# Scans without their empty ends, an output projection that begins with high parts, and two sums moved in the last FFN group

## The chip, the cores and the metric

The kernel is one program on one core of a Trainium2 chip. The metric is the device time of one execution in microseconds (us), median of three runs, lower is better. The engines are TensorE (PE, with its weight loads as PEld), VectorE (DVE), ScalarE (ACT), GpSimd (POOL) and SyncE (SP, which only issues DMAs here).

## The reference, cut to what matters

Two layers of a hybrid encoder trunk on x of shape 1 x 1024 x 1024, all in float32. One input projection feeds three mixers: a bidirectional Mamba-2 scan (8 heads of 64, state 128, chunks of 128 tokens, so 8 chunks), a gMLP spatial gate and a dilated attention. Their outputs are concatenated, go through an output projection, and a depthwise-conv gated FFN of width 2816 follows.

```python
def ssd_chunked(x, dt, a_neg, bm, cm):        # per direction; the backward one runs on flipped inputs
    ...
    states = jnp.einsum('bcsgn,bcsgh,bcsghp->bcghpn', bc, decay_out, xdt)
    def step(h, inp):
        st, dec = inp
        return h * dec[..., None, None] + st, h       # each chunk sees the state BEFORE it
    h0 = jnp.zeros((b, g, hg, p, n), jnp.float32)
    _, prev = lax.scan(step, h0, (states, chunk_decay))
    y_off = jnp.einsum('bctgn,bcghpn,bctgh->bctghp', cc, prev, jnp.exp(acs))
    return (y_diag + y_off)
...
y = y_fwd + y_bwd + d_skip * xs
y = rmsnorm(y * silu(z), out_gain)
x = x + concat(y_ssd, y_gmlp, y_attn) @ w_out
x = x + (silu(gate) * val) @ w_down                   # gate, val = dwconv(rmsnorm(x) @ w_up)
```

The state that the first chunk of a direction sees is zero, and the state after its last chunk is used by nobody.

## The kernel before, in words

Every float32 operand of a large matmul is held as a high part and a low part (HH and HL for activations, WH and WL for weights, AHI and ALO in the FFN), and a product is three matmuls: high by high, low by high, high by low (`mm3`, L484 to L488). The order of the work is written out by hand for each engine, and engines meet at counting semaphores. Weights arrive in units of 1 MB in two halves (SP, L369); POOL splits each half into WH (L474) and WL (L476), and two slots hold two units.

Per layer, the stages around the change are:

- **Backward scan.** Eight links i = 0 to 7, for chunk c = 7 - i. SP loads the chunk's tile (L433); tiles 4 and 5 go to the buffer XBS, tiles 6 and 7 to XBR, and between them SP issues the two halves of weight unit 13 and two gate tiles ZG (L400). PE transposes the tile (L742, `ra_turn`), ACT takes the B part (L1194), DVE makes XWA from it (L1608, `state_in`), PE multiplies the two (L753, `ra_state`), and DVE does BW[c] = BW[c+1] * decay (L1646) and BW[c] += that product (L1650). BW[8] and CURF are set to zero by two memsets (L1615, L1616). After link 4 DVE runs `far` (L1630, L1634), after link 5 `gate_sums` (L1624, L1626). PE then waits for the last L1650 (`ra_done`) before it transposes the first tile of the forward loop (L802).
- **Forward loop.** Eight chunks. DVE per chunk, in this order: XW (L1684), CURF * decay (L1687), Y1 from the forward state product in PSUM bank 5 (L1689), the gMLP sum GT (L1691, waits for PE L842), Y3 = XS * d_skip (L1694), the gMLP product (L1697), four operations on SEG (L1703, L1704), CURF += bank 7 (L1708), Y1 += Y3 (L1710), Y1 += Y2 (L1712), Y1 += bank 4 (L1717, waits for PE L869), and the gated product YT (L1719). PE per chunk: state products (L834, four for each direction), sums (L813, L818), gMLP (L842), the next tile's transposes (L802, L805), the new state (L856), and the diagonal product (L869, 16 matmuls). ACT: copies of XS and BC (L1234, L1238), exponentials (L1246), Y2 (L1255), sums of squares (L1216).
- **Turn and output projection.** For each 128-token tile c, DVE normalises (L1731), PE transposes (L888, `y_turn`), ACT copies the high part HH (L1268) and DVE subtracts for the low part HL (L1738, `low_part`). After `y_turn(0)` to `y_turn(3)` PE starts the first of 16 projection tiles (`columns_tile`), which waits for the low parts of four token tiles; `y_turn(4)` and `y_turn(5)` follow it, and `y_turn(6)` and `y_turn(7)` follow the second.
- **FFN.** 11 groups. A group's down projection is 16 fills of six matmuls each, rotating over PSUM banks 4 to 7. Fill i + 4 waits until DVE's `add(i)` (L1755) has taken bank 4 + i % 4 into X. In the last group (`g = NG - 1`) the adds of group NG - 2 are woven by hand between `conv_first` (L1773), `low` (L1791), `conv_last` (L1779) and `gated` (L1787).

Of the kernel before, what the change touches and what calls it, by code (L numbers as in the profile page):

```python
# [21 lines left out]
ALU = mybir.AluOpType  # L22
# [29 lines left out]
STEPS = NT * AH_  # L52
G_FIRST = 2 * KT
# [80 lines left out]
def trunk(nc, xT, wst, params, consts, onehot, lnrow, table, outT):  # L134
# [10 lines left out]
    with ExitStack() as ctx:  # L145
# [109 lines left out]
        BW = work("BW", [P, NT + 1, INNER])  # L255
# [107 lines left out]
        def _(sp):  # L363
# [39 lines left out]
            for l in range(DEPTH):  # L403
# [24 lines left out]
                for i in range(NT):  # L428
                    if i == 2:
                        sp.wait_ge(lg_ready, (l + 1) * STEPS)  # L430
                    if i >= 4:
                        sp.wait_ge(xbs_used, l * 2 * NT + i - 1)
# [8 lines left out]
                for c in range(NT):  # L441
                    sp.wait_ge(xbs_used, l * 2 * NT + (NT + 1 + c if c >= 2 else 7 + c))
# [37 lines left out]
        def _(pe):  # L480
# [24 lines left out]
            def norm_back(n, th):  # L505
# [5 lines left out]
                last.then_inc(ib_ready, 1)  # L511

# [90 lines left out]
            for l in range(DEPTH):  # L603
# [142 lines left out]
                def ra_state(i, par, first=False):  # L746
                    n = l * NT + i
# [20 lines left out]
                def tile_in(i):  # L768
                    pe.wait_ge(xbs_full[i % 4], 16 * (l * (6 if i % 4 < 2 else 2) + i // 4 + 1))
# [7 lines left out]
                pe.wait_ge(ra_t_full, l * NT + 1)  # L777
# [6 lines left out]
                pe.wait_ge(ra_t_full, l * NT + 2)  # L784
                pe.sem_inc(xbs_used, 1)
                for i in range(2, NT):
# [3 lines left out]
                    pe.wait_ge(ra_t_full, l * NT + i + 1)  # L790
                    pe.sem_inc(xbs_used, 1)
                    ra_state(i - 1, 1 - par)
                ra_state(NT - 1, 1)
# [3 lines left out]
                pe.wait_ge(ra_done, 1 + (l + 1) * NT)  # L797
# [24 lines left out]
                def chunk(i2, par, end):  # L822
# [3 lines left out]
                    pe.wait_ge(curf_ready, 1 + n)  # L826
                    pe.wait_ge(y12_done, 1 + n)
                    if n:
                        pe.wait_ge(y2_ready, n)
                    for d in range(2):  # L830
# [16 lines left out]

# [4 lines left out]
                    pe.wait_ge(bst_ready, n + 1)  # L852
                    pe.wait_ge(xw_ready, n + 1)
                    pe.wait_ge(gt_done, n + 1)
                    for g in range(GROUPS):
                        last = nc.tensor.matmul(PS[:, 7, g * 256:(g + 1) * 256], BC[:, 0, g, :],  # L856
                                                XW[:, g * 256:(g + 1) * 256], start=True, stop=True)
                    last.then_inc(sf_full, 1)
                    if not end:
                        sums(n + 1, 0)  # L860
                        sums(n + 1, 1)
# [32 lines left out]
                for i, (dt, th) in enumerate(W_ORDER):  # L894
# [11 lines left out]
                    if i < 2:  # L906
                        y_turn(4 + 2 * i)
                        y_turn(5 + 2 * i)
# [36 lines left out]
        def _(act):  # L945
# [85 lines left out]
            for l in range(DEPTH):  # L1031
# [159 lines left out]
                for i in range(NT):  # L1191
                    n, par = l * NT + i, i % 2
# [37 lines left out]
                for c in range(NT):  # L1230
# [5 lines left out]
                    if n:  # L1236
                        act.wait_ge(sf_full, n)
# [13 lines left out]
                    act.wait_ge(yo_full, n + 1)  # L1251
                    act.wait_ge(chunk_done, 1 + n)
                    for h in range(HEADS):
                        cols = slice(h * HD, (h + 1) * HD)
                        last = A(Y2[:, cols], PS[:, 6, cols], ACT.Copy, scale=EACS[:, c, 8 + h:9 + h])  # L1255
                    last.then_inc(y2_ready, 1)
# [58 lines left out]
        def _(dve):  # L1315
# [110 lines left out]
            for l in range(DEPTH):  # L1426
# [8 lines left out]
                dve.wait_ge(pad_zero, 6 * l + 1)  # L1435
# [51 lines left out]
                dve.wait_ge(pad_zero, 6 * l + 2)  # L1487
# [97 lines left out]
                dve.wait_ge(pad_zero, 6 * l + 3)  # L1585
# [19 lines left out]
                def state_in(i):  # L1605

                    dve.wait_ge(ra_t_full, l * NT + i + 1)
# [10 lines left out]
                dve.wait_ge(pad_zero, 6 * l + 5)  # L1618
# [19 lines left out]
                step = Steps(dve, ra_step, 1)  # L1638
                for i in range(NT):
                    n, par, c = l * NT + i, i % 2, NT - 1 - i  # L1640
                    step.begin(n)

                    if i + 1 < NT:
                        state_in(i + 1)
                    dve.wait_ge(ra_done, 1 + n)
                    step.then(TT(BW[:, c, :].rearrange("p (h e) -> p h e", h=HEADS),  # L1646
                                 BW[:, c + 1, :].rearrange("p (h e) -> p h e", h=HEADS), by_decay(CDEC, c), ALU.mult))
                    step.end()
                    dve.wait_ge(ra_s_full, n + 1)
                    TT(BW[:, c, :], BW[:, c, :], bank(2 + 3 * par), ALU.add).then_inc(ra_done, 1)  # L1650
                    if i == 4:
                        far()
                    if i == 5:
                        gate_sums()

# [12 lines left out]
                step = Steps(dve, chunk_step, 6)  # L1668
                for i2 in range(NT // 2):
                    for par in range(2):  # L1670
                        c = i2 * 2 + par
                        n = l * NT + c
                        step.begin(n)
# [10 lines left out]
                        TT(by_head(XW[:]), by_head(XS[:, par]), heads(WST, 0), ALU.mult).then_inc(xw_ready, 1)  # L1684

                        dve.wait_ge(yo_full, n + 1)
                        step.then(TT(by_head(CURF[:]), by_head(CURF[:]), heads(CDEC, 0), ALU.mult))  # L1687

# [248 lines left out]
```

## Time and profile before

| | |
|---|---|
| median of 3 runs | 2678.39 us (2677.86 to 2683.78) |
| profiled execution: own time, and its span | 2681.2 us, 2679.4 us |
| busy: PE, PEld, DVE, ACT, POOL | 2575.6, 2177.3, 1482.6, 896.7, 730.8 us |
| mean granted TensorE clock | 0.988 |
| layer 0: backward scan, forward loop, turn | about 407 to 430, 430 to 512, 512 to 523 us |
| layer 1: the same | about 1726 to 1748, 1748 to 1831, 1831 to 1841 us |

The span runs from the first to the last instruction of the profiled execution. Busy time is the union over an engine's instructions. A half-rate TensorE clock shows as a granted clock of 0.5 and as 128x512 matmuls of 0.63 us instead of 0.39 us. Matmuls overlap: at full rate one of 512 columns starts every 0.23 us. DVE operations overlap too, so their cost in a chain is the distance between starts, not their own duration.

### The profile page before, as it was taken

How to read it: one execution, taken by the hardware profiler on the slowest of the kernel's cores; microseconds unless marked ns; L12 is line 12 of the kernel's file. 1: busy time of each engine (PE TensorE's matmuls, PEld its weight loads, DVE VectorE, ACT ScalarE, POOL GpSimd, SP SyncE). 2: the span in 40 equal slices, each digit the busy share in tenths (PEclk: the TensorE clock that was granted, in tenths of full speed). 3: DMA queues.
4: the chain of work that ended last, by engine and by line, in shares of the span. 5: the costliest groups of instructions: out<-in, count | busy, mean ns of one | idle time of the engine just before them, and what ended most of it. 6: DMA issues, size and time to landing. Idle time of an engine off the chain costs nothing. (4 is left out here: it accounts for less than half of the span.)

```text
span 2679.4 us, 33472 instructions
## 1 busy us (share of the span) xinstructions
PE 2575.6 (96%) x13350; PEld 2177.3 (81%) x13350; DVE 1482.6 (55%) x1743; ACT 896.7 (33%) x1550; POOL 730.8 (27%) x388
## 2 busy tenths in 40 slices
PE   5999998899999999999999999988999999999998
PEld 5988986788888888888789889877888888888887
DVE  5376558837444444444575755696464444444445
ACT  3245556613222222222233465574132222222221
POOL 2332111024333333333323311100433333333331
PEclk8999999899999999999999999999999999999999
DMA  4443443121111111111123344521111111111111
GB/s 177 144 117 119 132 152 124 48 81 48 47 47 48 48 53 48 49 47 48 54 109 80 109 134 140 171 85 69 48 47 48 47 47 48 49 51 50 48 47 71
DMA packets 73725, 209.90 MB, mean 78 GB/s; under 512 B 5832, under 2 KB 28360, under 8 KB 72264
## 3 DMA queue, kind: packets, MB, share of 16 engines
q1 hardware_dynamic: 53384, 178.58, 20.3%
q10 hardware_dynamic: 20200, 29.30, 3.3%
q8 instruction: 106, 1.74, 0.3%
q14 instruction: 35, 0.29, 0.0%
HBM read 176.37 MB, written 31.49 MB: 78 GB/s over the span
## 5 line engine op out<-in xcount | busy, mean ns | idle before, releaser
L484 PE MATMUL PS<-HH,WH 128*128 128x512 f32 x1920 | 756.6, 394 | 4.9 <-issue 4.9
L474 POOL CAST WH<-RAW 128x1024 fp32r<-128x1024 f32 x192 | 238.7, 1243 | 1888.3 <-PE PS L484 1403.2
L488 PE MATMUL PS<-HH,WL 128*128 128x512 f32 x1920 | 753.3, 392 | 0.0
L487 PE MATMUL PS<-HL,WH 128*128 128x512 f32 x1920 | 753.2, 392 | 0.0
L476 POOL TENSOR_TENSOR WL<-RAW,WH 128x1024 fp32r<-128x1024 f32 x192 | 497.4, 2591 | 15.4
L1755 DVE TENSOR_TENSOR X<-PS,X 128x512 f32<-128x512 f32 x384 | 259.6, 689 | 378.7 <-PE PS L488 378.4
L484 PEld LDWEIGHTS PS<-HH,WH 128*128 128x128 f32 x1920 | 362.5, 189 | 84.3 <-issue 5.3
L488 PEld LDWEIGHTS PS<-HH,WL 128*128 128x128 f32 x1920 | 361.7, 188 | 81.3
L487 PEld LDWEIGHTS PS<-HL,WH 128*128 128x128 f32 x1920 | 362.2, 189 | 78.3
L1284 ACT ACTIVATE FPAD<-PS 128x512 f32<-128x512 f32 x176 | 102.6, 596 | 885.8 <-PE PS L488 885.8
L1773 DVE SCALAR_TENSOR_TENSOR CVV<-FPAD,PARM,CVV 128x1024 f32<-128x1024 f32 x44 | 95.3, 2166 | 377.8 <-ACT CVV L1290 377.8
L484 PE MATMUL PS<-AHI,WH 128*128 128x512 f32 x704 | 278.9, 396 | 4.9 <-DVE X L1755 4.9
L488 PE MATMUL PS<-AHI,WL 128*128 128x512 f32 x704 | 278.5, 396 | 0.0
L487 PE MATMUL PS<-ALO,WH 128*128 128x512 f32 x704 | 278.0, 395 | 0.0
L555 PE MATMUL PS<-WH,HH 128*128 128x256 f32 (+1 forms) x896 | 264.4, 295 | 12.7 <-DVE HL L1346 12.7
L558 PE MATMUL PS<-WL,HH 128*128 128x256 f32 (+1 forms) x896 | 256.9, 287 | 0.0
L559 PE MATMUL PS<-WH,HL 128*128 128x256 f32 (+1 forms) x896 | 256.9, 287 | 0.0
L555 PEld LDWEIGHTS PS<-WH,HH 128*128 128x128 f32 x896 | 174.1, 194 | 16.5 <-DVE HL L1346 9.0
L558 PEld LDWEIGHTS PS<-WL,HH 128*128 128x128 f32 x896 | 174.2, 194 | 0.1
L559 PEld LDWEIGHTS PS<-WH,HL 128*128 128x128 f32 x896 | 174.0, 194 | 0.0
L484 PEld LDWEIGHTS PS<-AHI,WH 128*128 128x128 f32 x704 | 133.1, 189 | 37.0 <-DVE X L1755 6.6
L488 PEld LDWEIGHTS PS<-AHI,WL 128*128 128x128 f32 x704 | 132.9, 189 | 31.3
(198 smaller groups left out, 3080.9 us busy)
## 6 DMA issues: line engine op xcount, KB each, us to landing
RAW<-wst SPq DMA_DIRECT2D x192, 512.0 KB, 3.5
TOE<-toe_d SPq DMA_DIRECT2D x64, 512.0 KB, 3.7
XBS<-xbc_d SPq DMA_DIRECT2D x24, 512.0 KB, 4.5
xspill<-X ACTq DMA_DIRECT2D x2, 4096.0 KB, 13.1
xbc_d<-CV ACTq DMA_DIRECT2D x16, 512.0 KB, 3.9
X<-xspill SPq DMA_DIRECT2D x4, 2048.0 KB, 7.3
tok_d<-ST ACTq DMA_DIRECT2D x12, 512.0 KB, 3.4
ZG<-tok_d SPq DMA_DIRECT2D x16, 384.0 KB, 3.6
```

The source lines that it names most:

```text
L474: nc.gpsimd.tensor_copy(hi, raw).then_inc(hi_done, 1)
L476: nc.gpsimd.tensor_tensor(lo, raw, hi.bitcast(F32), ALU.subtract).then_inc(w_ready, 1)
L484: ins = nc.tensor.matmul(out, wh, xh, start=first, stop=False)
L487: nc.tensor.matmul(out, wh, xl, start=False, stop=False)
L488: return nc.tensor.matmul(out, wl, xh, start=False, stop=last)
L555: ins = nc.tensor.matmul(o, xh, wh, start=(k == 0), stop=False)
L558: nc.tensor.matmul(o, xh, wl, start=False, stop=False)
L559: return nc.tensor.matmul(o, xl, wh, start=False, stop=(k == KT - 1))
L1284: A(FPAD[:, x % 2, 1 + th * HALF:1 + (th + 1) * HALF], bank(f % 4), ACT.Copy).then_inc(a_free, 1)
L1755: TT(x, bank(4 + i % 4), x, ALU.add).then_inc(b_free, 1)
L1773: step.then(STT(t, FPAD[:, x % 2, 0:SEQ], PARM[:, at:at + 1], t, ALU.mult, ALU.add))
```

## The change

The scans run over LINKS = NT - 1 = 7 links. The backward scan drops its eighth link (tile load, transposes, XWA, BSTA, product, L1646 and L1650), and its first link copies the product instead of multiplying a zero state and adding. The two memsets go. In the forward loop, chunk 0 has no forward state product, no L1687, L1689 and L1710, and copies bank 7 into CURF; chunk 7 has no backward state product, no XW, L1687, L856, L1708, Y2 and L1712. The first output-projection tile begins with its 16 matmuls on HH, then `y_turn(4)`, then its 8 on HL, then `y_turn(5)`. In the last FFN group two adds move ahead of each of three operations. Semaphore counts follow.

```diff
+LINKS = NT - 1
-        BW = work("BW", [P, NT + 1, INNER])
+        BW = work("BW", [P, NT, INNER])
# SP, PE, ACT, backward scan
-                for i in range(NT):
+                for i in range(LINKS):
...
# PE, first tile of the output projection
+            def columns_tile_late(s, ct, th, bank_n, low_ready):
+                tok = half(th)
+                for k in range(KT):
+                    wh, wl = wtile(s, k * UC + ct * P)
+                    nc.tensor.matmul(bank(bank_n), wh, HH[:, k, tok], start=(k == 0), stop=False)
+                    nc.tensor.matmul(bank(bank_n), wl, HH[:, k, tok], start=False, stop=False)
+                low_ready()
+                for k in range(KT):
+                    last = nc.tensor.matmul(bank(bank_n), wtile(s, k * UC + ct * P)[0], HL[:, k, tok], start=False,
+                                            stop=(k == KT - 1))
+                return last
...
-                    if i in (0, 4):
-                        pe.wait_ge(yl_ready, 2 + l * NT + 4 + i)
                     pe.wait_ge(b_free, BF + b0 + i + 1)
+                    if i == 0:
+                        pe.wait_ge(yh_ready, 1 + l * NT + 4)
+                        def low_ready():
+                            y_turn(4)
+                            pe.wait_ge(yl_ready, 2 + l * NT + 4)
+                        columns_tile_late(s, ct, th, 4, low_ready).then_inc(b_full, 1)
+                        y_turn(5)
+                        continue
+                    if i == 4:
+                        pe.wait_ge(yl_ready, 2 + l * NT + 8)
...
# PE, forward loop
-                    for d in range(2):
+                    for d in range(0 if c else 1, 1 if end else 2):
...
# DVE, backward scan
-                nc.vector.memset(BW[:, NT, :], 0.0).then_inc(pad_zero, 1)
-                nc.vector.memset(CURF[:], 0.0).then_inc(pad_zero, 1)
...
-                    step.then(TT(BW[:, c, :] ... BW[:, c + 1, :] ... by_decay(CDEC, c), ALU.mult))
+                    if i:
+                        dve.wait_ge(ra_done, 1 + n)
+                        step.then(TT(BW[:, c, :] ... BW[:, c + 1, :] ... by_decay(CDEC, c), ALU.mult))
                     dve.wait_ge(ra_s_full, n + 1)
-                    TT(BW[:, c, :], BW[:, c, :], bank(2 + 3 * par), ALU.add).then_inc(ra_done, 1)
+                    if i:
+                        ins = TT(BW[:, c, :], BW[:, c, :], bank(2 + 3 * par), ALU.add)
+                    else:
+                        ins = nc.vector.tensor_copy(BW[:, c, :], bank(2))
+                    ins.then_inc(ra_done, 1)
...
# DVE, forward loop: XW, L1708 and L1712 only if c < LINKS; L1687 only if 0 < c < LINKS; L1689 and L1710 only if c
-                        step.then(TT(by_head(Y3[:]), by_head(XS[:, par]), per_head(par_("d_skip")), ALU.mult))
+                        step.then(TT(by_head((Y3 if c else Y1)[:]), by_head(XS[:, par]), per_head(par_("d_skip")), ALU.mult))
...
# ACT, forward loop: Y2 (L1255) only if c < LINKS
# DVE, last FFN group
                 low(g, 0)
-                add(1, n0)
+                for i in range(1, 4):
+                    add(i, n0)
                 conv_last(g, 3)
-                for i in range(2, 4):
+                for i in range(4, 6):
                     add(i, n0)
                 gated(g, 1)
-                for i in range(4, 6):
+                for i in range(6, 8):
                     add(i, n0)
                 low(g, 1)
                 step.end()
-                for i in range(6, 16):
+                for i in range(8, 16):
                     add(i, n0)
```

## Rows read from the trace of the kernel before

**Rows 1.** The page, parts 1 and 2: busy times, and granted clock by slice.
```profile
PE 2575.6 (96%) x13350; PEld 2177.3 (81%) x13350; DVE 1482.6 (55%) x1743; ACT 896.7 (33%) x1550; POOL 730.8 (27%) x388
PEclk8999999899999999999999999999999999999999
```
**Rows 2.** Busy by stretch, forward loop: PE, PEld, DVE, ACT, POOL, clock, DMA, GB/s.
```profile
442.00:502.00 60.00, 55.69 (x341) 47.80 (x340) 57.57 (x95) 51.46 (x196) 0.00 (x0) 1.00 0.25 84
```
**Rows 3.** Timeline, DVE in the forward loop: start, us, engine, line, operation.
```profile
442.15 0.68 DVE L1710 TENSOR_TENSOR Y<-Y,Y 128x512 f32<-128x512 f32 x1
442.87 0.69 DVE L1712 TENSOR_TENSOR Y<-Y,Y 128x512 f32<-128x512 f32 x1
```
**Rows 4.** Timeline, backward scan of layer 0, idle before in brackets.
```profile
410.69 2.37 POOL L476 TENSOR_TENSOR WL<-RAW,WH 128x1024 fp32r<-128x1024 f32 x1
411.44 2.18 DVE L1646 TENSOR_TENSOR BW<-BW,CDEC 128x512 f32<-128x512 f32 x1
...
415.57 0.69 DVE L1650 TENSOR_TENSOR BW<-BW,PS 128x512 f32<-128x512 f32 x1
...
421.33 0.69 DVE L1650 TENSOR_TENSOR BW<-BW,PS 128x512 f32<-128x512 f32 x1
421.53 0.64 PEld L742 LDWEIGHTS PS<-CST,XBR 128*128 128x128 f32 x6 [1.66 <-DMA XBR<-xbc_d]
...
422.31 1.70 DVE L1634 SCALAR_TENSOR_TENSOR MHL<-PS,CST,MHL 64x256 fp32r<-64x256 f32 x4
...
429.75 0.88 PE L802 MATMUL PS<-CST,XBS 128*128 128x128 f32 x6 [1.62 <-DVE BW L1650]
```
**Rows 5.** Timeline, backward scan of layer 1, PE.
```profile
1740.33 0.88 PE L742 MATMUL PS<-CST,XBR 128*128 128x128 f32 x6 [1.78 <-DMA XBR<-xbc_d]
...
1748.05 0.88 PE L802 MATMUL PS<-CST,XBS 128*128 128x128 f32 x6 [1.62 <-DVE BW L1650]
```
**Rows 6.** Timeline, chunk 0 of layer 0, DVE.
```profile
437.50 0.42 DVE L1691 TENSOR_TENSOR GT<-PS,PARM 128x256 f32<-128x256 f32 x1 [2.31 <-PE PS L842]
```
**Rows 7.** Timeline, chunk 7 of layer 0.
```profile
502.88 1.00 PE L842 MATMUL PS<-ST,PARM 128*128 128x64 f32 x8
...
504.61 0.41 DVE L1691 TENSOR_TENSOR GT<-PS,PARM 128x256 f32<-128x256 f32 x1
...
507.56 3.65 PE L869 MATMUL PS<-XS,SEG 128*128 128x64 f32 x16 [1.28 <-DVE SEG L1704]
...
511.25 0.69 DVE L1717 TENSOR_TENSOR Y<-Y,PS 128x512 f32<-128x512 f32 x1
```
**Rows 8.** Timeline, end of the turn and start of the output projection, layer 0.
```profile
517.30 0.44 PE L888 MATMUL PS<-CST,YT 128*128 128x128 f32 x2 [0.67 <-DVE HL L1738]
...
520.71 1.02 ACT L1268 ACTIVATE HH<-PS 128x1024 fp32r<-128x1024 f32 x1 [0.90 <-PE PS L888]
...
521.79 1.22 DVE L1738 TENSOR_TENSOR HL<-PS,HH 128x1024 fp32r<-128x1024 f32 x1
...
523.12 0.47 PE L484 MATMUL PS<-HH,WH 128*128 128x512 f32 x1 [2.44 <-issue]
...
524.51 0.63 PE L488 MATMUL PS<-HH,WL 128*128 128x512 f32 x1
```
**Rows 9.** Timelines of POOL, DVE and PE, last FFN group of layer 0.
```profile
1313.36 3.24 POOL L476 TENSOR_TENSOR WL<-RAW,WH 128x1024 fp32r<-128x1024 f32 x1
...
1314.28 0.68 DVE L1755 TENSOR_TENSOR X<-PS,X 128x512 f32<-128x512 f32 x1
1314.88 2.79 DVE L1779 SCALAR_TENSOR_TENSOR CVV<-FPAD,PARM,CVV 128x1024 f32<-128x1024 f32 x1
1317.71 1.29 DVE L1755 TENSOR_TENSOR X<-PS,X 128x512 f32<-128x512 f32 x2
...
1318.46 0.50 PE L484 MATMUL PS<-AHI,WH 128*128 128x512 f32 x1 [1.77 <-DVE X L1755]
...
1320.83 0.63 PE L487 MATMUL PS<-ALO,WH 128*128 128x512 f32 x1
```

More of the change, by code:

```diff
@@ L824, in chunk @@
                     n = l * NT + c
[L826 to L829, printed above, removed]
-                    for d in range(2):
+                    if c:
+                        pe.wait_ge(curf_ready, 1 + l * LINKS + c)
+                        pe.wait_ge(y12_done, 1 + l * LINKS + c - 1)
+                    if not end:
+                        pe.wait_ge(y2_ready, l * LINKS + c)
+                    for d in range(0 if c else 1, 1 if end else 2):
                         for g in range(GROUPS):
@@ L851, in chunk @@
                         chunk_turn(i2, 1 - par)
[L852 to L859, printed above, removed]
+                        pe.wait_ge(bst_ready, n + 1)
+                        pe.wait_ge(xw_ready, l * LINKS + c + 1)
+                        pe.wait_ge(gt_done, n + 1)
+                        for g in range(GROUPS):
+                            last = nc.tensor.matmul(PS[:, 7, g * 256:(g + 1) * 256], BC[:, 0, g, :],
+                                                    XW[:, g * 256:(g + 1) * 256], start=True, stop=True)
+                        last.then_inc(sf_full, 1)
                         sums(n + 1, 0)
@@ L1250, in _ @@
                             v_scaled(c)
[L1251 to L1256, printed above, removed]
+                    if c < LINKS:
+                        act.wait_ge(yo_full, n + 1)
+                        act.wait_ge(chunk_done, 1 + n)
+                        for h in range(HEADS):
+                            cols = slice(h * HD, (h + 1) * HD)
+                            last = A(Y2[:, cols], PS[:, 6, cols], ACT.Copy, scale=EACS[:, c, 8 + h:9 + h])
+                        last.then_inc(y2_ready, 1)
                     if c:
@@ L1654, in _ @@
                         gate_sums()
+                step.end()
                 for q in range(2):
@@ L1667, in _ @@
                 dve.wait_ge(vr_ready, l + 1)
-                step = Steps(dve, chunk_step, 6)
+                step = Steps(dve, chunk_step, 6 * NT - 4)
+                step.begin(l)
                 for i2 in range(NT // 2):
@@ L1705, in _ @@
                                ALU.mult).then_inc(w_masked, 1)
-                        dve.wait_ge(sf_full, n + 1)
-                        TT(CURF[:], CURF[:], bank(7), ALU.add).then_inc(curf_ready, 1)
-                        dve.wait_ge(y12_done, 1 + n + 1)
-                        step.then(TT(Y1[:], Y1[:], Y3[:], ALU.add))
-                        dve.wait_ge(y2_ready, n + 1)
-                        step.then(TT(Y1[:], Y1[:], Y2[:], ALU.add))
+                        if c < LINKS:
+                            dve.wait_ge(sf_full, k + 1)
+                            if c:
+                                ins = TT(CURF[:], CURF[:], bank(7), ALU.add)
+                            else:
+                                ins = nc.vector.tensor_copy(CURF[:], bank(7))
+                            ins.then_inc(curf_ready, 1)
+                        if c:
+                            dve.wait_ge(y12_done, 1 + k)
+                            step.then(TT(Y1[:], Y1[:], Y3[:], ALU.add))
+                        if c < LINKS:
+                            dve.wait_ge(y2_ready, k + 1)
+                            step.then(TT(Y1[:], Y1[:], Y2[:], ALU.add))
                         if c == NT - 1:
@@ L1722, in _ @@
                         dve.sem_inc(zg_used, 1)
-                        step.end()
+                step.end()
                 def normalise(c):
```

73 lines of the change are left out of this document (36 added, 37 removed).

## Prediction, made before the changed kernel was run

> **What bounds the kernel now.** I read the page first. TensorE is busy 96% of the span and VectorE 55% [rows 1], so most of the kernel is TensorE's, and an edit elsewhere pays only in a stage where TensorE is not the bound. The slices of the granted clock show where such stages are: full or nearly full rate everywhere but at the start and in a few slices [rows 1]. I then asked for busy times by stretch. In 60 us of the forward loop DVE is busy 57.57 us [rows 2], and its operations start back to back, 0.72 us apart where both inputs are in SBUF [rows 3]; one that reads PSUM is followed after about 0.60 us, as the 1.29 us for two adds shows [rows 9]. So DVE sets the pace of that loop, and an operation taken out of it is worth its distance to the next. The backward scan is bound first by DVE and then by the landing of tile 6 (PE waited 1.66 us for it) and the chain behind that [rows 4]. The last FFN group is a TensorE stage with a hole: PE waited 1.77 us for an add on DVE [rows 9].
>
> All times below are of the profiled execution, 2681.2 us with a span of 2679.4. The median of the runs, 2678.39, is 2.8 us lower; I subtract the same saving from it.
>
> **A. Backward scan.** In layer 0, DVE starts the first decay product at 411.44 and it takes 2.18 us instead of the usual 0.68, ending after POOL's subtraction, which runs from 410.69 to 413.06 [rows 4]. The new kernel has no such product in link 0, only a copy, which the end of POOL's operation does not hold. The product of link 1 now comes early enough to meet it, ends near 413.7, and its add starts there instead of at 415.57 [rows 4]: 1.9 us earlier. The memsets vanish inside this same wait. Links 2 to 4 keep their pitch, so the add of link 4 starts at 419.4 instead of 421.33, and `far`, 2.1 us of DVE whose larger part is the 1.70 us of L1634 [rows 4], is over at about 422.1.
>
> Tile 6 does not come earlier. It stands in SP's queue behind the weight unit that waits for POOL, and neither moves; PE starts its transposes at 421.53 as before [rows 4]. From there: transposes and handover 0.9 us, XWA 0.6, decay product of link 5 0.7, add 0.6, `gate_sums` 0.3, decay product of link 6 0.7, add 0.7, handover 0.1, all DVE distances as in rows 3, with the two products on PE beside them: 4.7 us, so L802 starts near 426.3 instead of 429.75. That is 3.4 us. In layer 1 the same 4.7 to 4.8 us follow a landing at 1740.33 and replace 1748.05 - 1740.33 = 7.72 us [rows 5]: 2.9 us. The first forward tile was queued behind tile 7, which is gone, so it is not late. The floor is one link of two chained operations, 1.4 us per layer, if something else holds the chain after tile 6; the ceiling is the estimate plus 0.5.
>
> **B. Chunk 0.** DVE sat 2.31 us before GT, waiting for PE L842, which hangs on ACT's exponentials [rows 6]. L1687 and L1689 go from ahead of that wait and bring nothing. Behind it DVE is dense, so L1710 is worth its 0.72 us [rows 3]. The two copies replace adds that read the same bank. The trace has no such copy; I bound each between 0 and 0.7 us, where 0.7 is the whole of the add (0.69, L1650 in rows 4), and take the add's price, as the 512 elements read from PSUM are the same. Value 0.7 per layer.
>
> **C. Chunk 7.** XW and L1687 go ahead of GT: 0.61 + 0.72 = 1.3 us. But GT at 504.61 also waits for L842, which ran from 502.88 to 503.88 [rows 7]; with the four backward products gone it can end near 503.5, so only 1.1 us come through. Behind GT go L1708 (0.60) and L1712 (0.73): 1.3. Together 2.4 us, if TensorE's diagonal products keep up. They hardly do: L869 took 3.65 us for 16 small matmuls at half rate, and L1717 followed directly at 511.25 [rows 7]. In the new order DVE would be ready for it at 508.8. At half rate throughout, L869 ends near 510.1 and the gain is 1.1; at full rate it is 2.4. TensorE idles 3 us ahead of these matmuls in the new order, so the rate probably falls there again, somewhere along the 16. I take 1.6 per layer, ends 1.0 and 2.4. ACT's Y2 and the backward loads of PE lie beside DVE and count nothing.
>
> **D. Output projection.** PE began at 523.12, after the low part of tile 3 (521.79 + 1.22) [rows 8]. The new first tile needs only the high part, 520.71 + 1.02 = 521.73: 1.3 us earlier. It has 16 matmuls (3.7 us) before `y_turn(4)`, whose inputs were normalised by 522, and the low part is long there when the last 8 begin. The number of matmuls and transposes is the same, and from here on PE is the bound, so 1.3 us per layer stay.
>
> **The clock at that point.** From 524.1 to 527.5 the matmuls took 0.63 us (one in rows 8) and started 0.427 us apart instead of 0.233: 8 of them, 1.5 us lost, after PE had idled 2.44 us. In layer 1 it was 9. With an idle time of 1.1 us before the first matmul this may or may not recur; the rows don't decide it. I count one of the two layers, 1.5 us, ends 0 and 3.0. The Trainium skill (TensorE: Matmul & The Clock Gate, Part 4: PE-mode transpose) says that transposes do not count as PE-busy in the way other matmuls do. By that rule the turn's transposes would not hold the rate up and both half-rate stretches would stay, which makes this term 0 and the total 20.5. The trace disagrees in part: nothing but transposes ran from 511.0 on, and from 517.30 they ran at full rate, two in 0.44 us [rows 8].
>
> **E. Last FFN group.** DVE did `add(1)` at 1314.28, then `conv_last` for 2.79 us, and only then `add(2)` and `add(3)` at 1317.71; PE's fill 6 waited for `add(2)` until 1318.46 [rows 9]. `conv_last` was held by POOL's subtraction, which ended at 1316.60 (1313.36 + 3.24), 1.1 us before `conv_last` did, while the add, with its PSUM input, took its usual 0.68 in the same time [rows 9]. In the new order the adds 2 and 3 fill that hold, 1314.9 to 1316.1, and `conv_last` still ends near 1317.7: the move costs nothing. Fill 6 can follow fill 5 at 1316.5, 2.0 us earlier. Fills 8 and 9 need adds 4 and 5 by 1319.2 and 1320.6, and they are done by 1318.3 and 1318.9; 6 and 7 follow `gated`, in time for fills 10 and 11. `low(g, 1)`, which the last down projection needs, ends at 1322.5 as before, and PE gets there at 1327. If POOL's operation ended earlier, the two adds would push `conv_last` and all behind it by up to 1.2 us, which PE would still not feel before 1327.
>
> After this wait the matmuls ran at 0.63 us (one of nine in rows 9) from 1319.5 to 1322.9, which lost another 1.5 us. Without the wait I expect that stretch gone: the smaller wait before it alone had not lowered the rate. So 3.5 us per layer, ends 2.0 and 3.6.
>
> **Sum.** Layer 0: 3.4 + 0.7 + 1.6 + 1.3 + 3.5 = 10.5. Layer 1: 2.9 + 0.7 + 1.6 + 1.3 + 3.5 = 10.0. With 1.5 for the clock, 22.0 us. The profiled execution would be 2659.2, the median 2656.4.
>
> **Rivals.**
>
> 1. The clock gives nothing back. TensorE still idles before L869, before the projection and once in the last group; then terms D's clock (1.5) and E's clock (3.0) go and C falls to 1.1 twice (1.0). Gain 16.5, median 2662. For it: each of the half-rate stretches in these stages came after idle time of TensorE [rows 7 to 9], and some of that idle time remains. Against it: the largest waits shrink.
> 2. The backward scan keeps its end: after tile 6 something other than DVE's count, such as the next tile's landing or ACT's copies, holds the chain, and A brings only 1.4 per layer. Gain 22.0 - 3.5 = 18.5, median 2660. For it: PE did wait for DMA there in both layers [rows 4, 5]. Against: with tile 7 gone less is queued.
> 3. The change does less than it says: DVE's freed places in C are taken up by waits for PE and ACT, and only B, D and E's two waits pay, 0.7 + 1.3 + 2.0 per layer, while A gives 0. Then 8 us, median 2670; without D as well, 5.4, which is no change.
> 4. Slower: TensorE, with less to do in the scans, falls to half rate inside the forward loop. It is busy 55.69 of 60 us there at full rate [rows 2], so at half rate it becomes the bound; each such stretch costs about 1.5 us, as in rows 8 and 9. It decides from 22 / 1.5 = 15 stretches on. If it took half of the two loops, some 24, the time would be 2656.4 + 36 = 2692. Against it: chunks 1 to 6 lose no work on TensorE, and there was no half-rate stretch in the loop.
>
> **How the numbers follow.** Forecast 0.66, rival 1 0.17, rival 2 0.08, rival 3 0.06, rival 4 0.02, and 0.01 for gains beyond any of these. A measurement of this kernel can tell about 0.2%, 5.4 us, from no change. Low end: C at 2.4 twice (+1.6), clock at D 3.0 (+1.5), A at its ceiling (+1.0), and 1.5 for another stretch avoided by a shift in time: 27.6, so 2651. High end: past rival 1 with part of rival 2, a gain of 11.4, so 2667. Faster 0.93 (the forecast, rivals 1 and 2, and a third of rival 3), same 0.05, slower 0.02.
>
> **What would show it.** Right: layer 0, L802 of the first forward tile 4.7 us after the transposes of tile 6, against 8.2; the first matmul of the projection at the end of the fourth HH copy; no wait of PE over 1 us among the fills of the last group, and a granted clock of 1.0 there; fill 6 directly behind fill 5. Wrong: a chunk period in the loop other than the old 9.6 us; `conv_last` ending later than before relative to its fills; tile 6 landing later; a copy from PSUM that takes longer than the add; half-rate stretches in places that had none. The forecast fails as a whole if the loop's period grows by 2 us, as 12 inner chunks would then eat the 22 us.

## The result, and the profile after

The changed kernel took 2660.04 us in the median of 4 runs (2653.63 to 2661.84), the kernel before 2679.89 (4 runs). The ratio is 0.9928, 95% interval 0.9917 to 0.994: 19.9 us by the medians, where 22.0 had been forecast. Run again with more executions it gave 2657.13 against 2677.85, ratio 0.9931, interval 0.9916 to 0.9946, 20.7 us.

The page of the changed kernel, parts 1 and 2, beside [rows 1]:

```profile
PE 2564.2 (96%) x13306; PEld 2170.4 (82%) x13306; DVE 1462.5 (55%) x1717; ACT 892.6 (34%) x1532; POOL 730.0 (27%) x388
PEclk9999998999999999999999999998999999999999
```

TensorE lost 11.4 us of work, and the span lost 20.4. The rest is time in which TensorE had waited. But 3.1 of the 20.4 us are not the change's: they lie ahead of the first XWA of layer 0 (at 408.33 us before, at 405.21 now), where no computing instruction was changed. The granted clock was 0.50 there for 20.5 us before (from 36.0 and 66.7 us on) and for 10.2 us now. From that XWA on the trace of the changed kernel is 17.3 us shorter, and the second trace of it, further below, 19.2. The busy row of the forward loop beside [rows 2] shows that the loop itself is what it was:

```profile
442.00:502.00 60.00, 55.71 (x340) 47.45 (x338) 57.34 (x94) 51.03 (x195) 0.00 (x0) 1.00 0.25 84
```

Backward scan and chunk 0 of layer 0, POOL, DVE and PE, beside [rows 4] and [rows 6] (start, us, engine, line, operation, idle before in brackets; L477 is POOL's subtraction, L1673 the new copy, L1667 the decay product, L1671 the add, L756 the transposes, L767 the state product, L816 the first forward transposes, L832 a sum, L1717 GT):

```profile
407.58 2.38 POOL L477 TENSOR_TENSOR WL<-RAW,WH 128x1024 fp32r<-128x1024 f32 x1
408.41 0.69 DVE L1673 COPY BW<-PS 128x512 f32<-128x512 f32 x1 [0.42 <-PE PS L767]
...
409.67 0.83 DVE L1667 TENSOR_TENSOR BW<-BW,CDEC 128x512 f32<-128x512 f32 x1
410.54 0.69 DVE L1671 TENSOR_TENSOR BW<-BW,PS 128x512 f32<-128x512 f32 x1
...
416.72 0.69 DVE L1671 TENSOR_TENSOR BW<-BW,PS 128x512 f32<-128x512 f32 x1 [0.17 <-PE PS L767]
...
419.83 1.54 PE L756 MATMUL PS<-CST,XBR 128*128 128x128 f32 x6 [3.22 <-DMA XBR<-xbc_d]
421.67 3.75 PE L767 MATMUL PS<-XWA,BSTA 128*128 128x256 f32 x8 [0.31 <-PE PS L756]
...
426.28 0.88 PE L816 MATMUL PS<-CST,XBS 128*128 128x128 f32 x6 [0.85 <-DVE BW L1671]
...
433.02 0.63 PE L832 MATMUL PS<-MHL,SEL 128*128 128x512 f32 x1
...
435.35 0.42 DVE L1717 TENSOR_TENSOR GT<-PS,PARM 128x256 f32<-128x256 f32 x1 [6.16 <-PE PS L857]
```

The copy ran through POOL's subtraction unheld and took what the add did, 0.69 us. The product of link 1 is held for only 0.15 us (0.83 instead of 0.68), until POOL ends at 409.96. But tile 6 came late, six transposes took 1.54 us instead of 0.88 because the granted clock was 0.50 there (418.6 to 425.4 us), and it was 0.50 again in chunk 0 (432.2 to 439.1), where the sum L832 took 0.63 us instead of 0.39. Layer 1, beside [rows 5]:

```profile
1730.34 0.87 PE L756 MATMUL PS<-CST,XBR 128*128 128x128 f32 x6 [2.38 <-DMA XBR<-xbc_d]
...
1735.06 0.87 PE L816 MATMUL PS<-CST,XBS 128*128 128x128 f32 x6 [1.58 <-DVE BW L1671]
```

4.72 us lie between the two rows, where the forecast had 4.7 and before 7.72. Chunk 7 of layer 0 beside [rows 7], in the order of the timeline; L882 are the diagonal products, L1750 the add of their result:

```profile
501.81 0.42 DVE L1717 TENSOR_TENSOR GT<-PS,PARM 128x256 f32<-128x256 f32 x1
...
504.77 3.65 PE L882 MATMUL PS<-XS,SEG 128*128 128x64 f32 x16 [3.00 <-DVE SEG L1730]
...
508.46 0.69 DVE L1750 TENSOR_TENSOR Y<-Y,PS 128x512 f32<-128x512 f32 x1 [1.41 <-PE PS L882]
```

VectorE now waits 1.41 us for products that take 3.65 us, as before. Start of the projection, beside [rows 8]:

```profile
519.08 0.47 PE L519 MATMUL PS<-HH,WH 128*128 128x512 f32 x1 [1.21 <-ACT HH L1292]
519.39 0.39 PE L520 MATMUL PS<-HH,WL 128*128 128x512 f32 x1
```

It starts on the fourth HH copy, and at full rate. Last FFN group, beside [rows 9]; fill 5 is the first PE row and fill 6 the second:

```profile
1306.15 3.24 POOL L477 TENSOR_TENSOR WL<-RAW,WH 128x1024 fp32r<-128x1024 f32 x1
1307.07 1.87 DVE L1788 TENSOR_TENSOR X<-PS,X 128x512 f32<-128x512 f32 x3
1308.86 1.61 DVE L1812 SCALAR_TENSOR_TENSOR CVV<-FPAD,PARM,CVV 128x1024 f32<-128x1024 f32 x1
1310.51 1.29 DVE L1788 TENSOR_TENSOR X<-PS,X 128x512 f32<-128x512 f32 x2
```

```profile
1307.80 0.50 PE L485 MATMUL PS<-AHI,WH 128*128 128x512 f32 x1 [0.64 <-DVE X L1788]
...
1309.30 0.40 PE L485 MATMUL PS<-AHI,WH 128*128 128x512 f32 x1
```

`conv_last` (L1812) took 1.61 us instead of 2.79 and ended 1.1 us after POOL's subtraction, as before. The two adds stood in the time in which it was held before, and the only wait left is the small one of fill 5, 0.64 us.

### The profile page after: what moved, and what is told of

It reads as the page before. It is cut to its first block and busy times, and to the rows that moved or that the text cites. A ratio compares the mean times of both kernels' runs of the same rounds, so it can differ in the third digit from the quotient of the medians.

```text
span 2659.0 us, 33321 instructions
## 1 busy us (share of the span) xinstructions
PE 2564.2 (96%) x13306; PEld 2170.4 (82%) x13306; DVE 1462.5 (55%) x1717; ACT 892.6 (34%) x1532; POOL 730.0 (27%) x388
## 3 DMA queue, kind: packets, MB, share of 16 engines
q1 hardware_dynamic: 53096, 177.53, 20.4%
## 5 line engine op out<-in xcount | busy, mean ns | idle before, releaser
L485 PE MATMUL PS<-HH,WH 128*128 128x512 f32 x1904 | 748.5, 393 | 0.0
L488 PE MATMUL PS<-HL,WH 128*128 128x512 f32 x1904 | 745.2, 391 | 0.0
L489 PE MATMUL PS<-HH,WL 128*128 128x512 f32 x1904 | 745.0, 391 | 0.0
L477 POOL TENSOR_TENSOR WL<-RAW,WH 128x1024 fp32r<-128x1024 f32 x192 | 496.9, 2588 | 15.4
## 6 DMA issues: line engine op xcount, KB each, us to landing
xspill<-X ACTq DMA_DIRECT2D x2, 4096.0 KB, 13.1
```

The costliest lines, as they stand in the source:

```text
L477: nc.gpsimd.tensor_tensor(lo, raw, hi.bitcast(F32), ALU.subtract).then_inc(w_ready, 1)
L485: ins = nc.tensor.matmul(out, wh, xh, start=first, stop=False)
L488: nc.tensor.matmul(out, wh, xl, start=False, stop=False)
L489: return nc.tensor.matmul(out, wl, xh, start=False, stop=last)
```

## The experiments

A trace of one execution mixes the change with chance: over 24 runs the kernel before took 2673.69 to 2684.18 us. But every stage can be measured from one of its own instructions to the next, and those distances repeat to 0.05 us wherever the clock and the landing of tile 6 are the same. The table gives them for the two layers of each trace (us).

| kernel | scan | chunk 0 | loop | tail | turn | projection | last group |
|---|---|---|---|---|---|---|---|
| before | 21.4, 21.4 | 17.3, 17.3 | 57.5, 57.5 | 7.36, 7.12 | 11.2, 11.2 | 118.2, 118.2 | 26.9, 26.9 |
| projection only | 23.3, 21.4 | 17.7, 17.3 | 57.5, 57.5 | 7.12, 7.35 | 10.4, 9.9 | 116.5, 115.0 | 26.9, 25.4 |
| adds only | 23.1, 21.4 | 17.6, 17.4 | 57.5, 57.5 | 7.12, 7.35 | 11.6, 11.1 | 119.3, 118.2 | 23.3, 23.3 |
| fillers before projection | 21.7, 22.2 | 17.3, 17.6 | 57.5, 57.5 | 7.35, 7.11 | 11.1, 12.0 | 115.0, 114.9 | 26.9, 25.4 |
| scans only | 18.8, 19.8 | 16.7, 19.2 | 56.4, 56.4 | 6.92, 7.36 | 11.6, 11.1 | 119.1, 118.2 | 26.9, 26.9 |
| changed | 21.1, 18.5 | 19.1, 16.7 | 56.4, 56.4 | 7.36, 7.32 | 9.9, 10.4 | 115.0, 116.6 | 23.3, 23.3 |
| changed, again | 19.0, 18.0 | 17.8, 16.7 | 56.4, 56.4 | 7.36, 6.92 | 10.4, 10.4 | 116.9, 116.5 | 23.3, 23.3 |
| two idle operations | 18.5, 19.3 | 16.7, 17.6 | 56.4, 56.4 | 7.36, 7.36 | 10.4, 9.9 | 115.0, 115.0 | 23.3, 23.3 |
| fillers in chunk 7 | 19.0, 17.9 | 16.7, 17.6 | 56.4, 56.4 | 6.06, 6.06 | 10.4, 10.4 | 118.5, 116.6 | 23.3, 23.3 |
| tile 6 first | 17.9, 17.9 | 17.8, 16.7 | 56.4, 56.4 | 7.07, 6.93 | 10.4, 10.4 | 116.4, 116.5 | 23.3, 23.3 |
| all fillers | 17.9, 17.9 | 18.3, 16.7 | 56.4, 56.4 | 6.06, 6.06 | 10.4, 10.4 | 116.6, 118.6 | 23.3, 23.3 |
| tile 6, chunk 7 | 17.9, 17.9 | 16.7, 18.7 | 56.4, 56.4 | 6.06, 6.05 | 10.4, 10.4 | 116.8, 116.6 | 23.3, 23.3 |
| the same, far() late | 15.9, 15.9 | 17.7, 16.9 | 56.4, 56.4 | 6.06, 6.05 | 9.9, 10.3 | 116.6, 115.1 | 23.3, 23.3 |

Scan: first XWA to first forward transposes. Chunk 0: from there to GT of chunk 1. Loop: GT of chunk 1 to GT of chunk 7. Tail: from there to the last YT. Turn: to the first matmul of the projection. Projection: to the first ACT copy of the FFN. Last group: first fill of the down projection of group NG - 2 to that of group NG - 1. Between projection and last group lie 665.9 us in every trace. Fillers are matmuls whose result nobody uses; they only keep TensorE busy. Two stages stand outside the table. The time ahead of the first XWA runs from 400.1 to 408.3 us, with 3.4 to 20.5 us of granted clock 0.50 in its first 75 us. And from the last group of layer 0 to the first XWA of layer 1 it is 392.5 us before and 393.3 and 393.4 in the two traces of the changed kernel, with two half-rate stretches there (1350.4 and 1357.2 us in the first) where before has one (1367.2): another 0.8 us that the change did not keep.

**The parts alone.** The first kernel is the changed one without two of its edits; the other two are the kernel before with one edit each.

```diff
# scans_only = changed, minus (cut: the whole new first tile and the order of all moved adds)
-                        columns_tile_late(s, ct, th, 4, low_ready).then_inc(b_full, 1)
...
-                for i in range(1, 4):
-                    add(i, n0)
# proj_only = before + columns_tile_late and its turns; adds_only = before + the moved adds
```

> The changed kernel with the output projection and the last FFN group as before. The two traces so far show the forward scan part working (layer 1's backward scan 2.9 us shorter after tile 6, chunk 0 0.7, the wait before GT of chunk 7 1.1 shorter per layer), but the half of C behind GT (1.3 us) gone, because the diagonal products run at half rate. Theory 1 (each term as in the trace of the changed kernel: A 2.9, B 0.7, C 1.1 per layer, layer 0's A reduced by an occasional late landing of tile 6 or a half-rate stretch): 7 to 9.5 us under before. Theory 2 (my forecast's sizes hold on average and the one trace was unlucky): 3.2 + 0.7 + 1.6 per layer, 11 us. Theory 3 (the shorter scan only makes TensorE idle longer before tile 6, so the clock falls there regularly): 4 us or less, with half-rate stretches at the end of the backward scan in both layers.

Measured: 2670.45 against 2677.85, ratio 0.9971 (0.9961 to 0.9981), 7.4 us. Theory 1 holds in the sum, at its lower end; in this trace layer 1 lost 1.9 us in chunk 0 to the clock, where theory 1 had won 0.7. The stretches of theory 3 are there in both layers (granted clock 0.50 from 416.9 to 420.3 and from 1734.4 to 1737.8 us), but not its time: the scan is 2.6 and 1.6 us shorter than the 21.4 of before all the same.

> The kernel before with only the new first tile of the output projection. Term D: the first matmul comes 1.2 to 1.3 us earlier per layer, from the end of the fourth HH copy. Theory 1: with only half the idle time before it, the projection runs at full rate from its start, another 1.5 per layer: 5.5 us under before in all, no half-rate stretch at the start of the projection. Rival: the rate at that point depends on when the stretch falls and recurs in at least one layer: 2.5 to 4 us.

Measured: 2670.74, ratio 0.9971 (0.9962 to 0.998), 7.1 us: more than either theory. The turn ends 0.7 to 1.3 us earlier and the projection is 1.7 and 3.2 us shorter. Theory 1's "no half-rate stretch" failed in layer 0: the low clock, which had begun in the turn at 510.5 us, went on 3.3 us into the projection (L518 and L519 are the new tile):

```profile
524.23 0.77 PE L518 MATMUL PS<-HH,WH 128*128 128x512 f32 x1 [1.21 <-ACT HH L1291]
524.80 0.63 PE L519 MATMUL PS<-HH,WL 128*128 128x512 f32 x1
```

What neither theory had is that the later half-rate stretch of before, behind the FFN norm (from 626.5 and 1944.1 us on), is missing in both layers.

> The kernel before with only the adds moved in the last FFN group. Theory 1 (wait and clock both pay): 1.95 + 1.55 per layer, 7 us under before; no half-rate stretch in the last group in either layer. Rival (only the wait pays, the half-rate stretch stays): 3.9 us.

Measured: 2670.11, ratio 0.9972 (0.9961 to 0.9982), 7.7 us. The last group is 3.6 us shorter in both layers, as theory 1 says. The three parts alone sum to 22.2 us, the whole measured 20.7; there is no large effect of one part on another.

> The changed kernel unaltered, for a second trace and more times. If the late landing of tile 6 in layer 0 (14.6 us after the first XWA, against 13.2 before) and the half-rate stretch behind it belong to the change, they are there again; if they are chance, tile 6 comes 13.2 to 13.8 us after the first XWA in both layers and layer 0's L816 comes 2.5 us or more earlier relative to it than in the first trace. Time 18 to 22 us under before.

Measured: 20.7 us under before. Tile 6 came 14.0 and 13.3 us after the first XWA. The scan of layer 0 was 2.0 us shorter than in the first trace, not the 2.5 expected: half rate came again, 3.1 us before its end. A landing as late as 14.6 us was not seen again. Half-rate stretches at the end of the scan come without the change too: the kernels with the old scan have them in four of eight layers (23.3 and 23.1 in the table), those with the new scan in six of ten. The one of layer 0 in the first trace, 21.1, was the worst of ten layers with the new scan, whose mean is 19.0; the eight with the old one have 22.0.

**Why the tail did not shorten.** Two kernels, one that gives VectorE its removed work back and one that keeps TensorE busy.

```diff
# two_idle_ops: DVE, chunk 7
+                        if c == LINKS:
+                            nc.vector.tensor_copy(CURF[:], bank(7))
+                            TT(Y2[:], XS[:, par], XS[:, par], ALU.add)
# warm7: PE, chunk 7, ahead of the diagonal products of group g
+                        if end:
+                            if g == 0:
+                                pe.wait_ge(bst_ready, n + 1)
+                            for _ in range((12, 1)[g]):
+                                nc.tensor.matmul(bank(0), IDR[:, :], MHL[:, 0].rearrange("p h n -> p (h n)"),
+                                                 start=True, stop=True)
```

> The changed kernel, with a copy from PSUM and an add of SBUF operands, both without use, put back into VectorE's chunk 7 where the removed ones (L1708 and L1712 of before) stood: 0.60 + 0.72 us of VectorE time per layer. Theory (the half-rate diagonal products cover them): the step from GT to the last YT stays at 7.3 us where the clock is low, and the time is that of the changed kernel within 0.5 us. Rival (my term C as forecast): 0.5 us per layer or more is lost, and 1.3 if the loop's end is VectorE's.

Measured: 2654.98, ratio 0.9923 (0.9909 to 0.9937), so not slower than the changed kernel; the tail is 7.36 us in both layers, as in the changed kernel's own layers where the products ran at half rate from their start (7.36, 7.32 and 7.36; the fourth had 6.92). 1.32 us of VectorE per layer cost nothing there.

> The changed kernel, with 12 filler matmuls of 512 columns into an idle PSUM bank before the first diagonal products of chunk 7 and one before the second; their result is not used. Theory (C's second half is held by the half-rate clock of the diagonal products, not by their number): the products run at full rate, L882 takes about 2.3 us instead of 3.6, the step from GT to the last YT of chunk 7 falls from 7.3 to 5.9 us, 1.3 per layer, 2 to 3 us in all under the changed kernel. Rival (the products are held by something else, or the clock falls whatever TensorE does there): the step stays at 6.9 to 7.4 and the fillers cost up to 0.5 per layer.

Measured: 2654.08, ratio 0.9915 (0.9901 to 0.9929). The tail is 6.06 us in both layers, 1.3 less. Its timeline, PE, layer 0 (L883 fillers, L888 diagonal products):

```profile
493.85 3.01 PE L883 MATMUL PS<-MHL,IDR 128*128 128x512 f32 x12
496.95 1.10 PE L888 MATMUL PS<-XS,SEG 128*128 128x64 f32 x8
497.86 0.48 PE L883 MATMUL PS<-MHL,IDR 128*128 128x512 f32 x1
498.28 1.10 PE L888 MATMUL PS<-XS,SEG 128*128 128x64 f32 x8
```

Eight products in 1.10 us, full rate. So the number of products did not hold the tail, their clock did. The 1.3 us that come are the two removed operations of VectorE, 0.60 and 0.72 us; that they pay only when the clock stays up follows from the two kernels together, as no kernel had both the fillers and the two operations. In the whole time this is inside the noise: the kernel's interval overlaps the changed one's. In layer 0 of its trace the projection drew two half-rate stretches, one at its start and one behind the norm (118.5), where the traces of the changed kernel have at most one per layer.

**What ends the scan.** SP loads tile 6 before the weight unit instead of behind it and the gate tiles.

```diff
-                    if i == 5:
+                    if i == 6:
                         weights(l, 13, 14)
```

> The changed kernel, with SP loading tile 6 ahead of the weight unit and the two gate tiles instead of behind them. Theory (in the changed kernel the landing of tile 6 alone ends the backward scan): the wait of 2.8 to 3.6 us before its transposes goes, tile 6 is transposed 10.5 to 11.5 us after the first XWA instead of 13.8, and the scan is 2 to 3 us shorter per layer; no half-rate stretch at its end; 4 to 6 us under the changed kernel. Rival (the first forward tile and the gate tiles, which now land behind, take its place): the first forward transposes wait for their tile and less than 2 us comes in all.

Measured: 2655.11, ratio 0.9918 (0.9904 to 0.9931). Tile 6 is transposed after 11.24 us in both layers, and the scan takes 17.9 in both: 1.1 less than the mean of 19.0, not 2 to 3. In the whole time that is inside the noise, the interval overlaps the changed kernel's. What took the place of the landing is VectorE (the last add ends the wait of L816), and in layer 0 the half-rate clock came all the same:

```profile
418.60 1.10 PE L767 MATMUL PS<-XWA,BSTA 128*128 128x256 f32 x4 [1.55 <-issue]
421.48 1.54 PE L816 MATMUL PS<-CST,XBS 128*128 128x128 f32 x6 [1.77 <-DVE BW L1671]
```

> Tile 6 loaded first, the fillers of chunk 7, 7 more fillers in chunk 0 while TensorE waits for ScalarE's exponentials, and 6 in the first turn while it waits for the normalised tile. If idle time of TensorE is what lowers the clock at each of these places, no half-rate stretch is left between the backward scan and the FFN, GT of chunk 0 always comes 7.75 us after the first forward transposes, the fourth HH copy ends 9.7 us or less after the last YT, and the kernel is 8 to 11 us under the changed one, about 2647. If fillers don't hold the clock, it is at most 5 under.

Its extra edits were fillers like those of warm7 in chunk 0 (into bank 5) and in `y_turn(0)` (into bank 2). Measured: 2655.36, ratio 0.992 (0.9907 to 0.9934), which is wrong for the theory as I stated it. The 1.3 us of the tail came, the rest did not: the stretch of layer 0 had begun in the scan, ahead of the fillers, and at half rate seven fillers delayed GT of chunk 0 (9.37 us after the first transposes, where half rate without them gave 8.9 to 9.1). The turn did not shorten either: in spite of its fillers half rate began in both layers 13.1 and 13.8 us after GT of chunk 7, within the turn, and went on 3.4 and 4.2 us into the projection.

**What gave the projection its clock.** Fillers in the old order of the projection.

```diff
# proj_fill = before, ahead of the first projection tile
+                    if i == 0:
+                        pe.wait_ge(b_free, BF + b0 + i + 1)
+                        for _ in range(10):
+                            nc.tensor.matmul(bank(4), wtile(s, 0)[0], WH[:, W_AT[1]:W_AT[1] + HALF],
+                                             start=True, stop=True)
```

> The kernel before, with 10 filler matmuls of 512 columns (without use) ahead of the first projection tile, in the 2.5 us in which TensorE waits there for the low part of token tile 3; the order of the tile itself is the old one. Theory (the half-rate stretch at the start of the projection is due to that idle time, and the new order got rid of it by filling it): the first real matmul comes no earlier than before, but no half-rate stretch follows it, and the steps from it to the FFN are 116.5 or 115.0 us in place of 118.2: 1.5 to 3 us per layer, 3 to 5 us under before. Rival (the new order helps only by being early, or the transposes are what lowers the rate): the stretch stays and the time is that of before.

Measured: 2670.72 against 2678.28, ratio 0.9968 (0.9957 to 0.9979), 7.6 us, more than expected, with not one useful matmul earlier (L902 fillers, L484 the first of the tile):

```profile
520.62 2.53 PE L902 MATMUL PS<-WH 128*128 128x512 f32 x10
523.27 0.50 PE L484 MATMUL PS<-HH,WH 128*128 128x512 f32 x1
523.60 0.39 PE L487 MATMUL PS<-HL,WH 128*128 128x512 f32 x1
```

So filling TensorE's wait, and nothing else, removed that stretch: all six layers with the old tile and no fillers start the projection at half rate or fall to it within 1.0 us, neither of the two with fillers does. Two layers are few, but the time of seven runs says the same. The projection is 3.2 us shorter where one stretch explains 1.55: the second one, which before had after the FFN norm (a granted clock of 0.50 around 627 to 630 us), went too. Of ten layers with the new projection tile listed in the table up to "tile 6 first", without the fillers of chunk 7, four have 115.0 (neither stretch) and six 116.4 to 116.9. In five of these six (layer 0 of proj_only, both of after_again and of tile6_first) the half rate stands at the start of the projection, as the end of a low stretch that began in chunk 7 or the turn; in the sixth (layer 1 of the first trace) it stands behind the norm. None has both, as before has.

**A version that beats both.** With tile 6 early VectorE ends the scan, so its 2.1 us of `far` belong where it waits anyway.

```diff
# t6_warm7_far_late, on top of tile6_first and warm7 (t6_and_warm7)
-                    if i == 4:
-                        far()
...
                 step.end()
+                far()
# PE and ACT wait for far_ready only ahead of the first sums and the first exponential
```

> The changed kernel with tile 6 loaded first and the 12 + 1 fillers in chunk 7, the two edits that shortened their own stage: 17.9 us from the first XWA to the first forward transposes in both layers, GT to last YT in chunk 7 6.06 us. If the two add up, 1.1 + 1.25 per layer, 4.5 to 5 us under the changed kernel; if half-rate stretches only move on to other places, 2 or less.

Measured: 2653.27, ratio 0.9905 (0.989 to 0.992). Both stages keep their gain, 17.9 and 6.06, but layer 1 drew half rate in chunk 0 (18.7), and the interval still touches the changed kernel's.

> The same, and far() (2.1 us of VectorE between links 4 and 5 of the backward scan) moved behind the last link, where VectorE waits for ScalarE anyway. Theory (with tile 6 early, VectorE's chain is what ends the scan): 15.8 us from the first XWA to the first forward transposes, GT of chunk 0 still 7.8 us later (ScalarE's table load hides the later sums), another 2.1 per layer, 4 us, under the kernel beside it. Rival (TensorE's or ScalarE's part of a link is the bound, or GT of chunk 0 moves out by what was won): 1 us or less per layer.

Measured: 2645.71, ratio 0.9883 (0.9868 to 0.9898), 32.6 us under before and 7.6 under the kernel beside it. Its interval is clear of the changed kernel's. The scan takes 15.9 us in both layers, which is 4.0 of the 7.6 us; the trace shows the rest as half rate that it did not draw, above all 1.8 us in chunk 0 and 1.5 in the projection of layer 1, and as far as the runs show that is luck. VectorE, layer 0:

```profile
415.23 0.69 DVE L1678 TENSOR_TENSOR BW<-BW,PS 128x512 f32<-128x512 f32 x1
415.84 0.35 DVE L1658 TENSOR_SCALAR FAR<-CST 128x128 fp32r<-128x128 f32 x2
416.20 1.70 DVE L1662 SCALAR_TENSOR_TENSOR MHL<-PS,CST,MHL 64x256 fp32r<-64x256 f32 x4
...
424.76 0.42 DVE L1723 TENSOR_TENSOR GT<-PS,PARM 128x256 f32<-128x256 f32 x1 [3.85 <-PE PS L856]
```

The wait before GT is still 3.85 us (3.07 in layer 1), so the 2.1 us of `far` fit in it. GT came 8.8 and 8.0 us after the first transposes instead of 7.8. In layer 1 the granted clock was 1.00 from the scan to the end of the loop, so 0.2 of the 2.0 us are given back; the other 0.8 in layer 0 came with half rate from 422.9 us on, where the gMLP products L856 took 1.79 us instead of 1.00.

## Why the prediction was right, and where it was not

Means per layer, from the table (old against new edit, all traces that have the one or the other; the scan and chunk 0 with the old load order, the tail without fillers and idle operations, the projection without fillers in chunk 7 or ahead of it, the turn without fillers in it or behind it):

| term | forecast | measured | |
|---|---|---|---|
| A, scan | 3.4 and 2.9 | 22.0 to 19.0: 3.0 | right |
| B, chunk 0 | 0.7 | 17.4 to 17.5: 0.0 (0.6 at full rate) | eaten by the clock |
| C, ahead of GT | 1.1 | 57.5 to 56.4: 1.1 | right |
| C, behind GT | 0.5 | 7.24 to 7.16: 0.1 | mis-sized |
| D, start | 1.3 | turn 11.3 to 10.3: 1.0 | right |
| D, clock | 0.75 | projection 118.5 to 115.9: 2.6 | mis-sized |
| E | 3.5 | 26.5 to 23.3: 3.2 | right |
| sum | 11.0 | 11.0 | |

That the sum is 11.0 again is luck: B, C and the small shortfalls of A, D and E miss 1.85 us together, and the clock term of D is 1.85 too large. It is also a mean over all kernels. The changed kernel's own two traces gained 17.3 and 19.2 us from the first XWA on, not 22, and its runs 19.9 and 20.7. The time alone does not tell the forecast from rivals 1 and 2: the two intervals are gains of 16.1 to 22.2 and of 14.5 to 22.5 us, and 22.0, 18.5 and 16.5 lie in both. The stages tell them apart.

**A** went by its steps: the copy escaped POOL's hold, the add of link 1 moved up, tile 6 did not move, and 4.7 us follow it at full rate. The step "PE starts its transposes at 421.53 as before" holds on average only; the landing scatters over 13.0 to 14.6 us after the first XWA. The links in between did not keep their pitch (2.06 us instead of 1.92, with a wait of 0.17 for TensorE in each), which costs nothing as long as the landing is later. Rival 2 is out: wherever the clock was full, L816 came 4.73 us after the transposes of tile 6. That the landing of tile 6 bounds the scan was the forecast's own reading, and loading it first brought 1.1 us per layer on top.

**B.** "DVE is dense" behind GT, so L1710 pays 0.72: it does, from 9.59 to 8.90 us between GT 0 and GT 1, where the clock is full. In five of the ten layers with the new scan and the old load order it was not, against three of eight with the old one, and in the five chunk 0 took 0.3 to 1.9 us more than the old 17.3, in the three 0.3 at most. That is rival 4's mechanism at a small size and beside the loop, not in it, and one of the forecast's own signs of being wrong. Whether the new scan makes it more frequent, five of ten against three of eight can't say. Against its own full rate (16.7 us) a low clock costs the new chunk 0 0.9 to 2.5 us, the old one (17.3) 0.3: why it costs more was not tested.

**C, the step that failed** is "I take 1.6 per layer, ends 1.0 and 2.4". Ahead of GT the 1.1 us came to the hundredth. Behind it I let the diagonal products run partly at full rate. They ran at half rate through nearly all of their time in the first trace (tails of 7.36 and 7.32) and in one layer of the second (7.36; 6.92 in the other), and C as a whole came to 1.2, near its lower end of 1.0. The fillers of chunk 7, which left the products and VectorE's work as they were and gave 6.06, show that it was the clock.

**D** came nearly as forecast at its start, 1.0 us for 1.3. The term that was mis-sized is "I count one of the two layers, 1.5 us". It looked at the stretch at the start of the projection alone, and that one did what was forecast for it: it was gone in five of the ten layers with the new tile and still there in the other five. What the term left out is the second stretch, behind the norm, which before has in both layers, another 1.5 us each; nine of the ten layers lack it. The forecast had such a stretch only in its low end, as 1.5 us once. Together 2.6 us came instead of 0.75. proj_fill, which lost both stretches in both layers without one useful matmul earlier, points to TensorE's idle time ahead of the projection. Why the second stretch goes with it was not tested. By the rule of the Trainium skill that I weighed there (TensorE: Matmul & The Clock Gate, Part 4: PE-mode transpose) the stretches would have stayed in every layer. The traces agree with it only in part: five layers did start at half rate after a turn of nothing but transposes, but in the other five the granted clock rose to 1.00 within the turn (at 514.2 us in layer 0 of the first trace) and the projection started at full rate.

**E** by its steps: fill 6 follows fill 5 directly, 9.3 us after the first fill instead of 11.25, and the half-rate stretch behind the wait is gone (1.6 us). The mean is 3.2 instead of the 3.6 of most layers, because two of the eight old layers had no such stretch. `conv_last` ended with POOL's hold as computed.

Rival 1 was right of C's clock and wrong of D's and E's, which were its larger part. Rival 3 is out, as A and the half of C ahead of GT came, and so is rival 4, as every loop took 56.4 us.

## What to carry to other kernels

Price a removed operation by the wait that ends last behind it, and at the rate at which that engine will run then: taking work from one engine makes TensorE idle, and its next matmuls may run at half rate and eat the gain. In this kernel a wait of 1.8 to 2.4 us before a dense stretch of matmuls cost its own length and, in twelve of the fourteen places where the old order kept it (six at the projection, eight in the last group), about 1.5 us or more of half rate. Work that could be moved into it returned both; useless matmuls returned the 1.5 us only, and in the turn not even that. Compare stages from instruction to instruction within each trace: these distances repeat to 0.05 us at the same clock, where whole runs scatter by 10.

## What the hardware did that I had not expected

- Ten fillers in the old kernel, 2.5 us of TensorE work without use, made it 7.6 us faster (ratio 0.9968), as much as either of the real edits did alone.
- Fillers did not raise a clock that was already down: seven of them in chunk 0 ran at half rate and moved GT from 8.9 to 9.37 us.
- The landing of tile 6 behind a weight unit and two gate tiles varies by 1.7 us from layer to layer (13.0 to 14.6); loaded first it was transposed at 11.24 to 11.27 us in every one of eight layers.
